# First value projection from un-normalized features, bias rows on GpSimd, first weight tile by ScalarE's queue

## The chip, the core and the metric

The kernel runs on one NeuronCore of a Trainium2 chip. TensorE (PE) multiplies matrices out of SBUF into PSUM, VectorE (DVE) and ScalarE (ACT) work element by element, GpSimd (POOL) does so too and issues DMAs, SyncE (SP) issues DMAs. Each engine runs its own instructions in program order and waits on semaphores for the others. The metric is the device time of one execution, in microseconds.

## What is computed

A trunk of two layers over x of 512 tokens and 1024 features, in float32. Cut to what matters here:

```python
def rmsnorm(x, g):
    y = x * lax.rsqrt(jnp.mean(x * x, axis=-1, keepdims=True) + EPS)
    return y * g

# layer 0, hgrn2_mixer; u = rmsnorm(x, ln_g[0]), W = 2048
q, f_pre, i_in, gate = u @ w_in[:, 0:W], u @ w_in[:, W:2*W], u @ w_in[:, 2*W:3*W], u @ w_in[:, 3*W:4*W]
f = lb + (1.0 - lb) * sigmoid(f_pre)        # lb from a softmax over hg_lb_logits
# chunkwise recurrence with q, k = 1 - f, log f and the values i_in; then
y = rmsnorm_per_head(o) * norm_g * silu(gate);  h = x + y @ w_out
# layer 1: dilated attention in three groups; its logits get a relative-position bias
bias = bias_table[bucket]                   # bucket: distance -> one of 32, masked outside the window
```

Two facts carry the change. The norm multiplies a token's row by one number, its reciprocal root mean square, so `(x * g) @ w`, scaled by that number per token afterwards, is `rmsnorm(x, g) @ w`. And each row of the bias table is a piecewise constant function of distance.

## The kernel before

Features lie on partitions: `hT` holds x transposed as 8 slices (k = 0..7) of 128 features by 512 tokens, and `u` the normalized features in two parts, `u["hi"]` (rounded by ACT) and `u["lo"]` (the rest, by DVE). Weights come the same way: SP loads a tile of 512 KB to one of four slots of `raw`, ACT writes `w["hi"]`, DVE `w["lo"]`. A product is three matmuls, hi·hi, hi·lo and lo·hi (`split_matmuls`, L440).

The program is written by hand as one sequence for each engine, so the order in the source is the order on the engine. Layer 0 goes over 4 quads of 4 heads. For a head three tiles F, Q and G are projected (`head_tile`, weights stationary, 24 matmuls each in two halves); the values of a whole quad are projected by four tiles of two k each, into four PSUM banks, one for each block of 128 tokens (`value_step` for the first quad, `values` for later ones; u stationary, 3 matmuls for a k and a token block s, 96 in all). The recurrence of a head runs between the tiles of the next one: its scores, updates, outputs and norm sum stand in `recurrence`.

The opening, which the change is about, is one chain:

- SP loads x in four tiles `nat` (512 KB each, with `ident` behind the first), then the parameters, then four weight tiles, then constants, one-hot table, mask and bias table.
- PE transposes x, 32 transposes of 128x128 (L572) in eight groups of four, and DVE copies each group to `hT` (L1140). ACT squares x (L814) and computes the reciprocal root per token (L817, L819). DVE spreads it over a diagonal `y_f` (L1135), and PE makes `rstd` of it by a product with ones (L579).
- `norm(0)` on DVE: for each k, `tmp = hT * gain * rstd` (L1101) and `u["lo"] = tmp - u["hi"]` (L1106), with ACT's `u_high` (L791) between; the first four weight splits (`first_hi` L807, `first_lo` L1091) are woven in.
- PE starts the first values when slice 0 is split (`u_ready`), and in their middle multiplies the bias table by the one-hot table (`bias_rows`, L516). DVE adds the mask (L1174), SP stores the result to DRAM (`ext_rows`), and GpSimd writes the tiles of bias from there (L418).
- DVE computes the lower bound `lb` and `oml` from the parameters (L1148 to L1169).

`tmp` has two buffers, so slice k of `tmp` waits for `u["lo"]` of slice k-2. `qx` is scratch for mask and bias rows first, and belongs to `decays` (the recurrence's operands) afterwards; `load_after` on SP reloads a slot as soon as its two parts are made, and the store of `ext_rows` stands in SP's sequence behind the reloads of the first four slots.

## Time and profile before

| what | us |
|---|---|
| median of three runs | 1649.3 |
| lowest and highest | 1648.06, 1650.33 |
| the profiled execution | 1648.23 |
| its span, first to last instruction | 1646.4 |
| PE busy in the span | 1625.8 |
| DVE busy | 812.3 |
| ACT busy | 645.4 |
| POOL busy | 20.8 |

Between the span and the profiled execution's own time lie 1.8 us before and behind the recorded instructions. In the timeline a row stands for one instruction or for several alike, with its start, the time until the last of them ends, its engine, line and tiles, and in brackets how long the engine had been idle and what ended that. Matmul rows overlap: one of 0.39 us is followed by the next after 0.23 us. In names of products the moving operand comes first: `proj<-w_hi,u_hi` is a product of the values (u stationary), `proj<-u_hi,w_hi` one of a head tile.

### The profile page before, as it was taken

How to read it: one execution, taken by the hardware profiler on the slowest of the kernel's cores; microseconds unless marked ns; L12 is line 12 of the kernel's file. 1: busy time of each engine (PE TensorE's matmuls, PEld its weight loads, DVE VectorE, ACT ScalarE, POOL GpSimd, SP SyncE). 2: the span in 40 equal slices, each digit the busy share in tenths (PEclk: the TensorE clock that was granted, in tenths of full speed). 3: DMA queues.
4: the chain of work that ended last, by engine and by line, in shares of the span. 5: the costliest groups of instructions: out<-in, count | busy, mean ns of one | idle time of the engine just before them, and what ended most of it. 6: DMA issues, size and time to landing. Idle time of an engine off the chain costs nothing.

```text
span 1646.4 us, 22077 instructions
## 1 busy us (share of the span) xinstructions
PE 1625.8 (99%) x8235; PEld 1387.1 (84%) x8235; DVE 812.3 (49%) x1414; ACT 645.4 (39%) x1096; POOL 20.8 (1%) x40
## 2 busy tenths in 40 slices
PE   7999999999999999999999999999999999999997
PEld 5888888888887998888998888898888889888886
DVE  6674675575677724444333444423344431444445
ACT  4553453453453534333232334332333332243333
POOL 0000000000000000000000000000000000000000
PEclk9999999999999999999999999999999999999999
DMA  6523223323221433333232343333323333433311
GB/s 216 166 78 102 77 76 89 89 77 87 79 77 52 128 90 96 84 84 84 65 115 80 95 97 84 71 102 91 97 66 84 95 71 90 125 94 85 77 51 65
DMA packets 247998, 149.47 MB, mean 91 GB/s; under 512 B 47040, under 2 KB 227648, under 8 KB 247920
## 3 DMA queue, kind: packets, MB, share of 16 engines
q1 hardware_dynamic: 203328, 139.69, 30.6%
q0 software_dynamic: 2608, 8.39, 1.5%
q10 hardware_dynamic: 41984, 0.27, 1.3%
q8 instruction: 59, 0.97, 0.2%
q14 instruction: 19, 0.16, 0.0%
HBM read 146.02 MB, written 6.50 MB: 93 GB/s over the span
## 4 chain that ended last, share of the span: by engine, by line
PE 97%; DVE 2%; ACT 1%; DMA 0%; issue 0%; DVEq 0%; SPq 0%
PE proj L440 81%; PE inner L726 3%; PE inner L440 3%; PE inner L694 2%; PE inner L714 2%; PE inner L682 1%; PE inner L598 1%; PE inner L621 1%; PE inner L624 1%; PE inner L610 1%; PE inner L603 0%; DVE v L1532 0%; PE inner L631 0%; DMA ident<-consts 0%; DVE hT L1140 0%; PE inner L632 0%
## 5 line engine op out<-in xcount | busy, mean ns | idle before, releaser
L1086 DVE TENSOR_TENSOR w_lo<-raw,w_hi 128x1024 fp32r<-128x1024 f32 x252 | 307.8, 1223 | 451.0 <-ACT w_hi L775 449.9
L440 PE MATMUL proj<-u_hi,w_hi 128*128 128x512 f32 x1280 | 509.3, 398 | 0.0
L440 PE MATMUL proj<-u_hi,w_lo 128*128 128x512 f32 x1280 | 499.8, 390 | 0.0
L440 PE MATMUL proj<-u_lo,w_hi 128*128 128x512 f32 x1280 | 498.4, 389 | 0.0
L775 ACT ACTIVATE w_hi<-raw 128x1024 fp32r<-128x1024 f32 x252 | 265.0, 1053 | 127.8 <-PE proj L440 117.0
L440 PEld LDWEIGHTS proj<-u_hi,w_lo 128*128 128x128 f32 x1280 | 240.2, 188 | 52.0
L440 PEld LDWEIGHTS proj<-u_lo,w_hi 128*128 128x128 f32 x1280 | 240.7, 188 | 48.1
L440 PEld LDWEIGHTS proj<-u_hi,w_hi 128*128 128x128 f32 x1280 | 240.5, 188 | 47.8 <-issue 0.4
L440 PE MATMUL proj<-w_hi,u_hi 128*128 128x512 f32 x440 | 177.3, 403 | 3.0 <-DVE u_lo L1106 3.0
L440 PE MATMUL proj<-w_lo,u_hi 128*128 128x512 f32 x440 | 174.6, 397 | 0.0
L440 PE MATMUL proj<-w_hi,u_lo 128*128 128x512 f32 x440 | 174.4, 396 | 0.0
L440 PEld LDWEIGHTS proj<-w_hi,u_hi 128*128 128x128 f32 x440 | 113.8, 259 | 14.4 <-issue 4.5
L440 PEld LDWEIGHTS proj<-w_hi,u_lo 128*128 128x128 f32 x440 | 113.9, 259 | 8.0
L1032 ACT ACTIVATE qk<-proj 128x512 f32<-128x512 f32 x96 | 57.1, 595 | 161.6 <-PE proj L440 161.5
L440 PEld LDWEIGHTS proj<-w_lo,u_hi 128*128 128x128 f32 x440 | 114.1, 259 | 7.1
L962 ACT ACTIVATE rows<-rows,negm 128x256 f32<-128x256 f32 (+1 forms) x128 | 61.8, 484 | 141.5 <-DVE negm L1430 131.2
L440 PE MATMUL proj<-y_hi,w_hi 128*128 128x512 f32 x256 | 101.0, 394 | 1.2 <-DVE sg L1190 0.7
L440 PE MATMUL proj<-y_hi,w_lo 128*128 128x512 f32 x256 | 99.7, 390 | 0.0
L440 PE MATMUL proj<-y_lo,w_hi 128*128 128x512 f32 x256 | 99.7, 389 | 0.0
L1286 DVE TENSOR_TENSOR hT<-hT,proj 128x512 f32<-128x512 f32 x80 | 54.4, 686 | 63.7 <-PE proj L440 63.5
L783 ACT ACTIVATE v<-proj 128x512 f32<-128x512 f32 x52 | 31.0, 596 | 121.2 <-PE proj L440 109.8
L440 PEld LDWEIGHTS proj<-y_hi,w_hi 128*128 128x128 f32 x256 | 48.1, 188 | 12.0 <-issue 2.5
(172 smaller groups left out, 1490.1 us busy)
## 6 DMA issues: line engine op xcount, KB each, us to landing
raw<-at_w_in SPq DMA_DIRECT2D x160, 512.0 KB, 4.1
raw<-hg_w_in SPq DMA_DIRECT2D x64, 512.0 KB, 4.2
raw<-hg_w_out SPq DMA_DIRECT2D x16, 512.0 KB, 3.6
raw<-at_w_out SPq DMA_DIRECT2D x16, 512.0 KB, 4.8
v<-x SPq DMA_DIRECT2D x4, 512.0 KB, 5.0
bias_tiles<-ext_rows POOLq DMA_DIRECT2D x1, 2048.0 KB, 11.9
bias_tiles<-ext_rows POOLq DMA_DIRECT2D x2, 1024.0 KB, 17.2
bias_n<-bias_tiles POOLq DMA_DIRECT2D x16, 128.0 KB, 4.4
```

Source lines behind the costliest of these rows:

```text
L440: ins = nc.tensor.matmul(bank[:, :], stationary(a), moving(b), start=(first and n == 0), stop=(last and n == 2))
L598: ins = nc.tensor.matmul(to, aft[:, b * P + c * CH:b * P + (c + 1) * CH], q_steps(b, 0, c, NC - c), start=True, stop=True)
L610: ins = nc.tensor.matmul(p_U[:, b * P:(b + 1) * P], kT[:, b, :], v_sb[0][:, b, h * P:(h + 1) * P], start=True, stop=True)
L694: ins = nc.tensor.matmul(p_S[r // 2][:, ((r % 2) * 2 + i) * P:((r % 2) * 2 + i + 1) * P], qk[:, 2 + 2 * i, s], qk[:, 3 + 2 * i, s], start= ...
L714: ins = nc.tensor.transpose(p_T[n % 2][:, (i % 4) * P:(i % 4 + 1) * P], src, ident[:, :])
L726: ins = nc.tensor.matmul(o, vals, pT[:, i, :], start=(i == 0), stop=(i == len(TILES) - 1), skip_group_check=True)
L775: nc.scalar.activation(w["hi"][:, slot, :], raw[:, slot, :], ACT.Copy).then_inc(hi_ready, 1)
L783: nc.scalar.activation(v_sb[group][:, s, :], value_bank(layer, q, e)[:, :], ACT.Copy, scale=cols[:, 8 + ST * group + s:9 + ST * group + s] ...
L962: nc.scalar.activation(probs[:, i, 0:n], probs[:, i, 0:n], ACT.Exp, bias=negm[:, i:i + 1], accum_out=stat[:, i // ST, 1, b:b + 1]).then_in ...
L1032: nc.scalar.activation(o, src, ACT.Copy, scale=QSCALE if i in (Q0, Q1, Q2) else 1.0)\
L1086: nc.vector.tensor_tensor(w["lo"][:, slot, :], raw[:, slot, :], w["hi"][:, slot, :].bitcast(F32), ALU.subtract).then_inc(w_ready, 1)
L1286: nc.vector.tensor_tensor(hT[:, k, :], hT[:, k, :], proj[bank][:, :], ALU.add)\
```

## The change

- **Loads.** ACT's queue loads the first weight tile at its very start; SP loads x, `ident`, the gains `ln_g` behind `ident`, then the other three weight tiles, and the other parameters after them. The one-hot table is gone, the mask goes straight to `ext_sb`, and the bias table comes with heads on partitions (4-byte elements).
- **Copies.** Transposes are ordered by halves of the features: four groups with k = 0..3, then four with k = 4..7, and ACT, not DVE, copies them to `hT` (`x_copy`).
- **First values.** DVE makes `tmp = hT * gain` by blocks of 4 slices by 128 tokens (`x_gain`), ACT and DVE split them (`x_high`, `x_low`), and the first values are multiplied from these; `copy_values` scales them per token. PE runs 7 + 8 + 2 products of ones into a bank that nobody reads, before and between the first transposes.
- **Norm behind it.** `norm(0)` runs as before, but each pair of slices of `u` is written only when the values' tile that reads it is done. Splits of the next weight tiles, `lb` and `oml` stand in or behind it. The first head tile waits for each slice (`u_ready`).
- **Bias rows.** GpSimd adds the bias, one instruction for each run of equal bucket (53 runs on 16 partitions by 1 to 30 elements), to the mask in place; `bias_rows` and DVE's three additions are gone. `decays` waits for the store of these rows.

```diff
@@ sync
             load_x(0)
             sp.dma_start(ident[:, :], consts[:, 0:P]).then_inc(const_loaded[0], 16)
+            sp.dma_start(prow[0:16, P:2 * P], ln_g.rearrange("r (h p) -> (r h) p", p=P)).then_inc(const_loaded[3], 16)
             for t in range(1, ST):
                 load_x(t)
+            for n in range(1, SLOTS):
+                load(n, *tile_source(HG, 0, "value", 0, n))
...
-                    sp.wait_ge(ext_ready, GROUPS)
+                    sp.wait_ge(ext_ready, 1)
@@ gpsimd
+            pool.wait_ge(const_loaded[5], 16)
+            pool.wait_ge(const_loaded[6], 16)
+            for g, bucket, first, count, step in bias_runs():
+                run = slice(g * EXT + first, g * EXT + first + (count - 1) * step + 1, step)
+                ins = nc.gpsimd.tensor_scalar(ext_sb[:, run], ext_sb[:, run],
+                                              relb_sb[:, bucket * GROUPS + g:bucket * GROUPS + g + 1], None, ALU.add)
+            ins.then_inc(ext_ready, 1)
@@ tensor, value_step
-                if s == 0 and layer is HG:
-                    pe.wait_ge(u_ready, k + 1)
+                if layer is HG and k % 4 == 0:
+                    pe.wait_ge(raw_ready, k + s + 1)
@@ scalar
             def u_high(which, k):
-                if which:
-                    wait_tile_done(act, AT, None, 4 + k // 2, False)
+                wait_tile_done(act, AT if which else HG, None, 4 * which + k // 2, False)
...
+            act.dma_start(raw[:, 0, :].rearrange("p (k n) -> p k n", k=2),
+                          w_in[HG][:, 0:2, HG_VALUE[0]:HG_VALUE[0] + HQ * P]).then_inc(loaded[0], 16)
...
+            x_square(0)
+            x_copy(0)
+            first_hi(0)
+            x_high(0)
+            x_copy(1)
+            x_copy(2)
+            x_high(1)
+            first_hi(1)
+            x_copy(3)
+            x_high(2)
+            x_high(3)
+            x_square(1)
+            x_copy(4)
+            x_square(2)
+            x_square(3)
...
+            x_copy(5)
+            x_high(4)
@@ vector, norm
+                    if not which and k == 2:
+                        split_lo(HG, None, 0, False)
+                    if not which and k == KT - 2:
+                        split_lo(HG, None, 1, False)
+                        split_lo(HG, None, 2, False)
+                        dve.wait_ge(param_T, 1)
+                        nc.vector.tensor_copy(param[:, 0:64], inner[1][:, 0:64]).then_inc(param_ready, 1)
...
+            def x_gain(n):
+                half = n // ST
+                dve.wait_ge(x_copied, n + 1)
+                if n >= 2:
+                    dve.wait_ge(raw_ready, n - 1)
+                nc.vector.tensor_tensor(tmp[:, n % 2, :].rearrange("p (a b) -> p a b", b=P), block(hT, n),
+                                        param[:, 64 + 4 * half:68 + 4 * half].unsqueeze(2).broadcast_to([P, 4, P]),
+                                        ALU.mult).then_inc(xg_made, 1)
...
@@ vector, decays
                 dve.wait_ge(eb_ready, 2 * g + 2)
+                dve.wait_ge(ext_stored, 16)
```

PE's sequence at its start, before. `v` is x as loaded, `inner` and `proj` are PSUM banks:

```order
L572 MATMUL inner<-ident,v 128x128 x32
L576 MATMUL proj<-ident,rows 128x80
L579 MATMUL inner<-y_f,ones 128x512
L440 MATMUL proj<-w_hi,u_hi 128x512
L440 MATMUL proj<-w_lo,u_hi 128x512
L440 MATMUL proj<-w_hi,u_lo 128x512
```

And PE's sequence at the same place in the changed kernel (L448 is `split_matmuls`, L582 the transposes, L567 and L572 the products of ones):

```order
L567 MATMUL proj<-ones 128x128 x7
L582 MATMUL inner<-ident,v 128x128 x4
L588 MATMUL inner<-ident,rows 128x16
L572 MATMUL proj<-ones 128x128 x8
L582 MATMUL inner<-ident,v 128x128 x4
L572 MATMUL proj<-ones 128x128 x2
L582 MATMUL inner<-ident,v 128x128 x4
L448 MATMUL proj<-w_hi,u_hi 128x512
L448 MATMUL proj<-w_lo,u_hi 128x512
L448 MATMUL proj<-w_hi,u_lo 128x512
```

The products of the values now stand behind twelve transposes where thirty-two stood before, and the other twenty, with the product that makes `rstd`, stand between them.

DVE's sequence behind its first copies, before, up to the second split of a weight tile:

```order
L1143 COPY param<-proj 128x80
L1091 TENSOR_TENSOR w_lo<-raw,w_hi 128x1024
L1101 SCALAR_TENSOR_TENSOR tmp<-hT,param,rstd 128x512 x2
L1106 TENSOR_TENSOR u_lo<-tmp,u_hi 128x512
L1101 SCALAR_TENSOR_TENSOR tmp<-hT,param,rstd 128x512
L1106 TENSOR_TENSOR u_lo<-tmp,u_hi 128x512
L1091 TENSOR_TENSOR w_lo<-raw,w_hi 128x1024
```

DVE's sequence in the changed kernel from block 5 of `x_gain` to the start of `norm(0)` (L1217 `x_gain`, L1224 `x_low`, L1163 `first_lo`, L1173 the first step of the norm):

```order
L1217 TENSOR_TENSOR tmp<-hT,param 128x512 x2
L1224 TENSOR_TENSOR u_lo<-tmp,u_hi 128x4x128
L1244 TENSOR_TENSOR y_f<-ident,cols 128x512
L1217 TENSOR_TENSOR tmp<-hT,param 128x512
L1224 TENSOR_TENSOR u_lo<-tmp,u_hi 128x4x128
L1217 TENSOR_TENSOR tmp<-hT,param 128x512
L1224 TENSOR_TENSOR u_lo<-tmp,u_hi 128x4x128
L1163 TENSOR_TENSOR w_lo<-raw,w_hi 128x1024
L1224 TENSOR_TENSOR u_lo<-tmp,u_hi 128x4x128
L1163 TENSOR_TENSOR w_lo<-raw,w_hi 128x1024
L1173 SCALAR_TENSOR_TENSOR tmp<-hT,param,rstd 128x512 x2
```

The norm, which stood almost first on DVE, now stands behind sixteen block operations, four splits and the diagonal.

## Rows read from the trace of the kernel before

**Rows 1.** The page, part 1 (PE, DVE, POOL) and part 4 (the chain that ended last).

```profile
PE 1625.8 (99%) x8235; PEld 1387.1 (84%) x8235; DVE 812.3 (49%) x1414; ACT 645.4 (39%) x1096; POOL 20.8 (1%) x40
...
PE 97%; DVE 2%; ACT 1%; DMA 0%; issue 0%; DVEq 0%; SPq 0%
```

**Rows 2.** Windows: stretch, length, busy of each engine, granted clock, DMA share, GB/s.

```profile
8.00:15.50 7.50, 3.56 (x23) 2.53 (x22) 7.40 (x12) 5.03 (x10) 0.00 (x0) 0.97 1.06 368
15.50:21.80 6.30, 5.85 (x14) 4.62 (x15) 6.23 (x9) 3.85 (x6) 0.00 (x0) 0.50 0.70 163
21.80:43.00 21.20, 21.20 (x91) 16.04 (x90) 13.28 (x27) 7.93 (x12) 3.23 (x3) 1.00 0.57 176
```

**Rows 3.** Timeline: loads of x, squares on ACT, transposes, and the product for `rstd`.

```profile
0.88 0.39 SPq L364 DMA_DIRECT2D v<-x  x1
...
4.94 1.06 ACT L814 ACTIVATE qk<-v 128x1024 f32<-128x1024 f32 x1 [2.77 <-DMA v<-x]
...
5.19 5.17 PE L572 MATMUL inner<-ident,v 128*128 128x128 f32 x32 [5.19 <-DMA ident<-consts]
...
5.90 0.19 ACT L814 ACTIVATION_READ_ACCUMULATOR qk<-v 128x1 f32 x1
...
9.03 1.06 ACT L814 ACTIVATE rows<-v 128x1024 f32<-128x1024 f32 x1 [0.22 <-DMA v<-x]
...
11.79 1.13 PE L579 MATMUL inner<-y_f,ones 128*128 128x512 f32 x2 [1.36 <-DVE y_f L1135]
```

**Rows 4.** Timeline: the first slice's split, the first product of the values, and its successor.

```profile
15.11 0.69 DVE L1106 TENSOR_TENSOR u_lo<-tmp,u_hi 128x512 fp32r<-128x512 f32 x1
15.65 1.05 ACT L807 ACTIVATE w_hi<-raw 128x1024 fp32r<-128x1024 f32 x1
15.84 0.75 DVE L1101 SCALAR_TENSOR_TENSOR tmp<-hT,param,rstd 128x512 f32<-128x512 f32 x1
...
15.95 0.76 PE L440 MATMUL proj<-w_hi,u_hi 128*128 128x512 f32 x1 [3.04 <-DVE u_lo L1106]
...
16.51 0.68 DVE L1106 TENSOR_TENSOR u_lo<-tmp,u_hi 128x512 fp32r<-128x512 f32 x1
...
16.63 0.63 ACT L791 ACTIVATE u_hi<-tmp 128x512 fp32r<-128x512 f32 x1
...
17.12 1.22 DVE L1091 TENSOR_TENSOR w_lo<-raw,w_hi 128x1024 fp32r<-128x1024 f32 x1
```

**Rows 5.** Timeline: first and last DVE steps of the norm.

```profile
13.67 1.41 DVE L1101 SCALAR_TENSOR_TENSOR tmp<-hT,param,rstd 128x512 f32<-128x512 f32 x2
...
26.49 1.48 DVE L1106 TENSOR_TENSOR u_lo<-tmp,u_hi 128x512 fp32r<-128x512 f32 x2
```

**Rows 6.** Timeline: the values' product ahead of the bias rows and the one behind them.

```profile
29.50 0.39 PE L440 MATMUL inner<-w_hi,u_lo 128*128 128x512 f32 x1
...
31.85 0.50 PE L440 MATMUL proj<-w_hi,u_hi 128*128 128x512 f32 x1
```

**Rows 7.** Timeline: PE begins the first and the second head tile.

```profile
42.91 0.39 PE L440 MATMUL proj<-u_hi,w_hi 128*128 128x512 f32 x1
...
48.35 0.39 PE L440 MATMUL proj<-u_hi,w_hi 128*128 128x512 f32 x1
```

**Rows 8.** Timeline: GpSimd's only instructions that write SBUF.

```profile
0.48 0.10 POOL L1569 MEMSET const-uint8-127<- 128x1 uint8 x1
0.87 0.20 POOL L406 MEMSET ones<- 128x128 f32 x1 [0.29 <-POOLq L1569]
```

**Rows 9.** Timeline: first recurrence, on DVE its operands, on PE its scores.

```profile
54.98 0.69 DVE L1242 TENSOR_TENSOR qx<-proj,rows 128x512 f32<-128x512 f32 x1
...
58.43 0.42 DVE L1255 TENSOR_TENSOR qx<-qx,rows 128x256 f32<-128x256 f32 x1
...
62.04 1.06 PE L598 MATMUL inner<-qx,aft 128*32 128x128 f32 x32
```

**Rows 10.** DMA issues: the last constants and the store of bias rows, us to landing.

```profile
bias_n<-rel_bias SPq DMA_DIRECT2D x1, 6.0 KB, 9.0
...
ext_rows<-qx SPq DMA_DIRECT2D x1, 72.0 KB, 2.0
```

More of the change, by code:

```diff
@@ L23 @@
+import itertools
 from contextlib import ExitStack
@@ L563, in _ @@
             pe.wait_ge(ones_ready, 1)
+            for _ in range(7):
+                nc.tensor.matmul(proj[2][:, 0:P], ones[:, :], ones[:, :], start=True, stop=True)
             pe.wait_ge(const_loaded[0], 16)
[L565 to L573 removed]
@@ L574, in _, with idle_products, x_transposes @@
-            for i in (1, 2, 3):
-                pe.wait_ge(const_loaded[i], 16)
-            nc.tensor.transpose(proj[0][:, 0:80], prow[0:80, 0:P], ident[0:80, 0:80]).then_inc(param_T, 1)
+            def idle_products(n):
+                for _ in range(n):
+                    nc.tensor.matmul(proj[2][:, 0:P], ones[:, :], ones[:, :], start=True, stop=True)
+            def x_transposes(half, t):
+                n = ST * half + t
+                if half == 0:
+                    pe.wait_ge(x_loaded[t], 16)
+                if n >= 3:
+                    pe.wait_ge(x_copied, n - 2)
+                for i in range(4):
+                    ins = nc.tensor.transpose(inner[1 + n % 3][:, i * P:(i + 1) * P],
+                                              nat[t][:, half, i * P:(i + 1) * P], ident[:, :])
+                ins.then_inc(x_T, 1)
@@ L647, in hg_body @@
                     for half in range(2 * HG.per_head):
-                        head_tile(HG, q, HG.per_head * h + half // 2, half % 2)
+                        head_tile(HG, q, HG.per_head * h + half // 2, half % 2, first=(h == 0 and half < 2))
                         if h:
@@ new lines, in x_low @@
+            def x_low(n):
+                dve.wait_ge(raw_hi_ready, n + 1)
+                nc.vector.tensor_tensor(block(u["lo"], n), tmp[:, n % 2, :].rearrange("p (a b) -> p a b", b=P),
+                                        block(u["hi"], n).bitcast(F32), ALU.subtract).then_inc(raw_ready, 1)
+            dve.wait_ge(gain_T, 1)
+            nc.vector.tensor_copy(param[:, 64:80], p_ss[:, 64:80]).then_inc(gain_ready, 1)
+            dve.wait_ge(gain_ready, 1)
+            x_gain(0)
+            first_lo(0)
@@ L1145, in _ @@
+            x_gain(6)
+            x_low(5)
+            x_gain(7)
+            x_low(6)
+            first_lo(2)
+            x_low(7)
+            first_lo(3)
+            dve.wait_ge(raw_ready, KT)
+            norm(0)
             dve.wait_ge(param_ready, 1)
-            norm(0)
             nc.vector.tensor_tensor(lb[:, :], param[:, 0:H], param[:, H:2 * H], ALU.max).then_inc(lb_step, 1)
@@ L1543, in bucket_of, with distance, bias_runs @@
     return np.where(dist < exact, dist, np.minimum(large, BUCKETS - 1))
+def distance(g, e):
+    window, dilation = ((128, 1), (512, 4), (2048, 16))[g]
+    apart = 2 * P - 1 - e
+    dist = apart * (1 if g == 0 else RES)
+    return dist if apart >= 0 and dist % dilation == 0 and dist <= window else None
+def bias_runs():
+    for g in range(GROUPS):
+        step = RES if g == 2 else 1
+        seen = [e for e in range(EXT) if distance(g, e) is not None]
+        for bucket, run in itertools.groupby(seen, lambda e: int(bucket_of(np.array(distance(g, e))))):
+            run = list(run)
+            assert run == list(range(run[0], run[-1] + 1, step))
+            yield g, bucket, run[0], len(run), step
 def shape_constants():
@@ L1551, in shape_constants @@
     consts[:, 2 * P:] = (np.arange(S) % CH != 0)
-    onehot = np.zeros((BUCKETS, GROUPS, EXT), np.float32)
     relmask = np.full((H, GROUPS, EXT), MASKED, np.float32)
-    for g, (window, dilation) in enumerate(((128, 1), (512, 4), (2048, 16))):
-        order = 1 if g == 0 else RES
+    for g in range(GROUPS):
         for e in range(EXT):
-            apart = 2 * P - 1 - e
-            dist = apart * order
-            if apart >= 0 and dist % dilation == 0 and dist <= window:
-                onehot[bucket_of(np.array(dist)), g, e] = 1.0
+            if distance(g, e) is not None:
                 relmask[:, g, e] = 0.0
-    return consts, onehot.reshape(BUCKETS, -1), relmask.reshape(H, -1)
+    return consts, relmask.reshape(H, -1)
 def kernel(**inputs):
```

181 lines of the change are left out of this document (103 added, 78 removed).

## The prediction, made before the changed kernel ran

> **What bounds the kernel now.** The page first: PE is busy for 99% of the span and is 97% of the chain that ended last [rows 1]. A microsecond that PE gains at the start is one for the kernel, as long as what follows doesn't wait for something else; DVE and ACT, each under half busy over the whole, can bound it only locally. So I read the opening in the timeline. PE transposes from 5.19 as x lands [rows 3], and begins the values only at 15.95, 0.15 after DVE has split the first slice (15.11 + 0.69) [rows 4]. From there it has no gap but one of bias rows until the head tiles, which begin at 42.91 and 48.35 [rows 7]. Those two starts are my markers: all that the change touches lies before 48.35, and behind it both kernels do the same matmuls. The windows show the clock [rows 2]: granted 0.97 up to 15.5, when PE had been idle for most of 5 us, then 0.50 (the lower level, 1.2 GHz) for 6.3 us with 14 products, then 1.00 (2.4 GHz). At full clock a product of 512 columns follows another after 0.227 us ((48.35 - 42.91) / 24) [rows 7]; in the slow stretch it took 5.85 / 14 = 0.42 [rows 2].
>
> **Steps on each engine.** Rows of one instruction overlap the next by a tenth, so I price by starts. DVE by 512 elements: 0.61 to 0.67, I take 0.65 (15.84 to 16.51 to 17.12); DVE by 1024: 1.22, 1.17 as a step; ACT by 512: 0.63, a step of 0.57; ACT by 1024: 0.98 (15.65 to 16.63) [rows 4]. A square with its sum: 5.90 + 0.19 - 4.94 = 1.15, I take 1.2 [rows 3]. Four transposes: 5.17 / 8 = 0.65 while PE also waited for copies; I take 0.5 [rows 3].
>
> **Loads.** x(0) was issued at 0.88 and ACT had it at 4.94; x(3) came at 9.03, so 512 KB take (9.03 - 4.94) / 3 = 1.36 us with the DMA engines full [rows 3]. The changed kernel issues the first weight tile at the same moment from another queue. The DMA share was 1.06 of the engines in the stretch around the loads [rows 2], so nothing is left to share out: the two together take 2.7 us where one took 1.3, and x(0) lands between 4.94 (it goes ahead) and 6.3. I take 6.2, because both queues start at once, and the weights land with it. The Trainium skill, "DMA: Bandwidth & Descriptors", section "Issuing engines are not separate DMA queues", says that DMAs of all issuing engines run on the same 16 and interleave; by that rule too x(0) is late, and if it did not hold, x(0) would stay at 4.94 and the total below 1.3 us lower.
>
> **ACT up to the second half of x.** In its order: square, copy (7.4 to 8.0), first weight split (to 9.0), `x_high(0)` (to 9.5), and on the other side DVE's `x_gain(0)` at 8.05, the weight's low part (to 10.2), `x_low(0)` (to 10.85). So PE's first product of the values is at 10.98: 4.97 earlier than 15.95. But ACT has more ahead of the second half: up to the end of `x_copy(5)` 4 squares (4.8), 6 copies and 4 `x_high` (5.7), 2 weight splits (2.0), one small one (0.3) and some 1.05 of waits for DVE and PE: 6.2 + 13.9 = 20.1.
>
> **DVE from there.** `x_gain(5)` must wait for that copy. Then DVE has 8 steps of 0.65 and 2 of 1.17 to the start of the norm: 20.1 + 7.6 = 27.7. The norm is the same chain as before, 8 steps of `tmp`, 8 of `u["lo"]`, 3 weight splits: it took from 13.67 to 26.49 + 1.48 = 27.97, that is 14.3 [rows 5], with a copy of parameters (0.2) now 14.5. It ends at 42.3, and slice 6, one step ahead of the last, is split at 41.7.
>
> **PE.** From 10.98: eight value steps of 3 products (5.5), transposes between them (4 groups, 2.0), waits for `x_low` of 0.45, then k = 2 with the last group (3.2), the product for `rstd` (1.0; it took 1.13 [rows 3]) and a wait of 0.1, twenty value steps (13.6), one small transpose (0.15): 37.05, where the first head tile can begin. Before it was 42.91. As a sum of differences: the start -4.97; the slow clock, if it doesn't return, 14 x (0.42 - 0.227) = -2.7 [rows 2]; bias rows gone from PE, -(31.85 - 29.50 - 0.23) = -2.1 [rows 6]; five groups of transposes +2.5, the product and small transpose +1.2, waits +0.55. That is -5.5 by rounded terms, -5.86 laid out step by step; the difference is in PE's first products at the change of clock. Now the norm comes too: the head tile wants slice 6 at 37.05 + 18 x 0.227 = 41.15 and gets it at 41.83 (41.7 and a hop), a stall of 0.7. The second head tile begins at 37.05 + 5.45 + 0.7 = 43.2 instead of 48.35: **-5.15 us without any interference**. DVE is from here the bound: each microsecond that it loses in the norm is lost one for one.
>
> **GpSimd beside DVE.** 53 instructions start when mask and bias table have landed. The bias table came 9.0 after its issue at 8.72 [rows 10], so about 17.5. No row shows such an instruction, nor DVE beside it. The nearest are memsets: 0.10 for one column, 0.20 for 128 [rows 8]. If they share nothing with DVE the cost is 0. If each takes something from DVE, 53 x 0.10 = 5.3 us is the row's upper figure if all of it fell on DVE, and twice that by the other memset. I expect a part only: DVE idles from about 17.5 to 20.1, where a good number go free, and of the rest each DVE step meets at most one. I take 0.05 on each of the 28 large steps from 20.1 to 42: +1.4. It can't be below nothing, since nothing leaves DVE's norm for it (the three additions came behind the norm).
> The Trainium skill speaks against this part: "SBUF — State Buffer", section "Who interferes with whom", has VectorE instructions with two SBUF inputs and GpSimd instructions that read SBUF exclude each other for a whole instruction, whichever began first. All of DVE's block and norm steps have two such inputs. No row here shows it; by the rule the term is above zero, without it the sum would be -5.15.
>
> **What costs nothing.** The products of ones run while PE would wait for x and for `x_low(0)`: 17 small ones, 3.6 us at full clock, in a stretch that begins at 1.1 and has PE idle for 4; if that cover is gone (x lands at 4.94) the eight of them delay the second transposes by under 1 us, with ACT not yet there. The eight waits on `u_ready` at each quad's first tile ride on matmuls and are long fulfilled. The store wait in `decays` stands ahead of all of DVE's recurrence: it needs GpSimd done and 2.0 us for the store [rows 10]. `decays` began at 54.98 [rows 9]; everything being earlier, it comes now at about 52.4 by DVE's own order (the lower bound, one split and a memset moved behind the norm delay it by some 2.5 us against the head tile). Scores were wanted at 62.04 and their operands were ready at 58.43 + 0.42 = 58.85 [rows 9], a reserve of 3.2. Of it 2.5 are used up; 0.7 stay.
>
> **The time.** -5.15 + 1.4 = -3.75. The profiled execution took 1648.23, 1.1 under the median of 1649.3; the difference goes against either alike: 1648.23 - 3.75 = 1644.5, and 1649.3 - 3.75 = 1645.55. I state the latter.
>
> **Rivals.**
> 1. *The full gain.* GpSimd takes nothing from DVE: -5.15, 1644.15; with x(0) at 4.94 it is -6.4, 1642.9. For it: sixteen partitions and few elements. Against: nothing measured either way. Chance 0.22.
> 2. *The forecast*, -2.9 to -4.6: 1644.7 to 1646.4. Chance 0.38.
> 3. *DVE loses 0.1 or more per step, or the clock falls again.* At 0.1 on 28 steps it is +2.8, -2.35, 1646.95; at 0.2, +5.6, +0.45, 1649.75. If PE is granted 0.5 for a stretch like the one before while it works on the values, it loses up to 2.7 us, 0.7 of which the stall of the first head tile absorbs: -3.1 alone, -1.9 with a little of the other. For it: between 5.19 and 15.5 PE's work was nearly all transposes and the clock fell behind it [rows 2, 3]; the same kind of work with pauses precedes the values now. Against: 17 real products were added among them, and the idle stretch is shorter. 1646.4 to 1650. Chance 0.30.
> 4. *Slower: GpSimd holds SP and DVE.* The store of bias rows waits for all 53; SP's next weight load stands behind it, and `decays` in DVE. It decides where `ext_ready` comes later than about 50: (50 - 17.5) / 53 = 0.6 us for each instruction. If each has to wait behind a DVE step of 0.65 to 1.17 and DVE leaves no pause, that is the rate; at 1.0 they end at 70.5, the store at 72.5, and the recurrence is 20 us late, of which the reserve covers 0.7: +19 - 5, 1663. The same rival in a milder form is a DVE loss of 0.3 per step: +8.4 - 5.15 = +3.3, 1652.6. Against: DVE is nearly idle after 45 and GpSimd catches up. Chance 0.07.
> 5. *It isn't kept.* The recurrence of the first head, started 2.5 us later against its tiles, makes PE wait and gives back 1 to 3: -1 to -3, 1646.3 to 1648.3. Chance 0.03.
>
> **Range and chances.** 0.2% of 1649.3, 3.3 us, is about what a measurement can tell from no change. Rival 1 and the better 0.30 or so of the forecast are beyond it: faster 0.52. The rest of the forecast, most of rival 3 and rival 5: same 0.40. Slower 0.08. The range leaves out rival 4, half of the ends of 1 and 3: 1642.9 to 1649.3.
>
> **What would show it.** PE's first values product near 11.0 and x(0) seen by ACT near 6.2; no stretch at 0.5 after 11; DVE's norm from 27.7 to 42 or a little more, steps of 0.70 instead of 0.65 while GpSimd works; head tiles at 37 and 44.6 on PE, the stall in the first before its slices 6 and 7; `ext_rows` stored before 50; scores of the first head without a wait. The prediction is wrong if DVE's steps beside GpSimd take 0.8 and more, if the granted clock is 0.5 while the values run, or if the second head tile is early and the span isn't.

## The result

The changed kernel takes 1657.6 us (median of five runs, 1656.1 to 1658.1) against 1649.3: 1.0050 of the kernel before, 95% interval 1.0036 to 1.0064. It is slower by 8.3 us. The profiled execution has a span of 1656.2 where the kernel before had 1646.4, 9.8 more. Parts 1 and 4 of its page, to be read beside [rows 1]:

```profile
PE 1629.7 (98%) x8264; PEld 1391.0 (84%) x8264; DVE 816.2 (49%) x1420; ACT 653.6 (39%) x1112; POOL 54.1 (3%) x93
...
PE 93%; POOL 2%; DMA 2%; DVE 2%; ACT 1%; SPq 1%; issue 0%; DVEq 0%
```

GpSimd is busy 33 us longer, and 2% of the chain that ended last, some 33 us, lie on it. Nothing of it stood on that chain before. Yet the opening came out near the forecast, in part by errors that cancel (see below). The timeline of the changed kernel, the rows that answer to [rows 3, 4, 7]:

```profile
4.88 1.06 ACT L862 ACTIVATE qk<-v 128x1024 f32<-128x1024 f32 x1 [2.21 <-DMA v<-x]
...
10.27 0.47 PE L448 MATMUL proj<-w_hi,u_hi 128*128 128x512 f32 x1
...
38.03 0.50 PE L448 MATMUL proj<-u_hi,w_hi 128*128 128x512 f32 x1 [0.81 <-ACT v L816]
...
43.60 0.39 PE L448 MATMUL proj<-u_hi,w_hi 128*128 128x512 f32 x1
```

The values begin at 10.27 instead of 15.95, the second head tile at 43.60 instead of 48.35: 4.75 us won. What came then is in the windows (stretch, length, busy of PE, PEld, DVE, ACT, POOL, granted clock, DMA share, GB/s):

```profile
46.00:52.00 6.00, 6.00 (x29) 4.95 (x28) 1.15 (x3) 1.36 (x2) 6.00 (x20) 1.00 0.01 3
52.00:58.00 6.00, 5.37 (x24) 4.12 (x22) 0.00 (x0) 0.09 (x1) 3.60 (x6) 1.00 0.59 157
58.00:64.00 6.00, 0.00 (x0) 0.00 (x0) 4.35 (x7) 4.06 (x6) 0.35 (x1) 0.61 1.08 360
64.00:70.00 6.00, 4.12 (x40) 3.40 (x41) 4.96 (x12) 1.79 (x3) 0.00 (x0) 0.54 0.97 315
```

From 52 to 58 DVE and ACT do nothing, from 58 to 64 PE does nothing, and behind it the granted clock is at its lower level. DMA moves 3 GB/s from 46 to 52: no weight tile is on its way. The timeline tells why (GpSimd's additions and SP's store, the loads behind it, ACT and DVE waiting, and PE's scores):

```profile
19.53 4.76 POOL L420 TENSOR_SCALAR qx<-qx,bias_n 16x30 f32<-16x30 f32 x5 [18.44 <-DMA bias_n<-rel_bias]
...
52.67 0.34 SPq L385 DMA_DIRECT2D ext_rows<-qx  x1
53.45 28.61 SPq L342 DMA_DIRECT2D raw<-hg_w_in  x8
...
57.91 1.06 ACT L808 ACTIVATE w_hi<-raw 128x1024 fp32r<-128x1024 f32 x1 [10.30 <-DMA raw<-hg_w_in]
...
59.51 1.23 DVE L1332 TENSOR_TENSOR_SCAN rows<-restart,rows 128x512 f32<-128x512 f32 x1 [10.73 <-ACT rows L980]
...
65.88 1.92 PE L631 MATMUL inner<-qx,aft 128*32 128x128 f32 x32 [8.51 <-DVE qx L1357]
```

The 53 additions last from 19.53 to the store at 52.67, 0.62 us each. SP waits for them, and its next weight load, behind that wait, goes out at 53.45. ACT's split of that tile stands ahead of its logarithm of the forget gate, which DVE's scan needs, which the scores need. In the kernel before, the scores stood at 62.04 without a wait [rows 9]. Here 4.75 us of lead turned into 3.84 of lag. The second head's scores come at 92.54 against 82.70 (PE, the kernel before and then the changed one):

```profile
82.70 1.06 PE L598 MATMUL inner<-qx,aft 128*32 128x128 f32 x32
```

```profile
82.09 0.50 PE L664 MATMUL inner<-osq_hi,ones_r 128*128 128x512 f32 x1 [2.47 <-DVE osq_lo L1371]
...
92.54 1.06 PE L631 MATMUL inner<-qx,aft 128*32 128x128 f32 x32
```

So 6.0 us more were lost between the two, 2.5 of them as a wait of the first norm sum, and the rest behind the two waits, where the granted clock is low (0.54 from 64 to 70 above, 0.72 from 82 to 88). From there the two kernels run alike: 9.84 at these scores, 9.8 at the end.

This gives a reading that serves for every run below: the start of the second head tile says what the opening is worth, and the span less that start what was lost behind it. Both come from one profiled execution, the median from all. It is 1598.05 for the kernel before and 1612.6 for the changed one.

### The profile page after: what moved, and what is told of

Its sections match the earlier page's. It is cut to its first block, busy times and chain, and to the rows that moved or that the text cites. A ratio compares the mean times of both kernels' runs of the same rounds, so it can differ in the third digit from the quotient of the medians.

```text
span 1656.2 us, 22236 instructions
## 1 busy us (share of the span) xinstructions
PE 1629.7 (98%) x8264; PEld 1391.0 (84%) x8264; DVE 816.2 (49%) x1420; ACT 653.6 (39%) x1112; POOL 54.1 (3%) x93
## 4 chain that ended last, share of the span: by engine, by line
PE 93%; POOL 2%; DMA 2%; DVE 2%; ACT 1%; SPq 1%; issue 0%; DVEq 0%
PE proj L448 78%; PE inner L759 3%; PE inner L448 3%; POOL qx L420 2%; PE inner L727 2%; PE inner L747 2%; PE inner L715 1%; DMA raw<-hg_w_in 1%; PE inner L631 1%; PE inner L654 1%; DMA bias_n<-rel_bias 1%; PE inner L657 1%; PE inner L643 1%; PE inner L636 0%; DVE v L1634 0%
## 5 line engine op out<-in xcount | busy, mean ns | idle before, releaser
L448 PE MATMUL proj<-u_hi,w_hi 128*128 128x512 f32 x1280 | 510.4, 399 | 0.8 <-ACT v L816 0.8
L448 PE MATMUL proj<-u_hi,w_lo 128*128 128x512 f32 x1280 | 500.5, 391 | 0.0
L448 PE MATMUL proj<-u_lo,w_hi 128*128 128x512 f32 x1280 | 499.2, 390 | 0.0
L448 PEld LDWEIGHTS proj<-u_hi,w_lo 128*128 128x128 f32 x1280 | 240.8, 188 | 52.3
L448 PEld LDWEIGHTS proj<-u_hi,w_hi 128*128 128x128 f32 x1280 | 241.1, 188 | 48.9 <-ACT v L816 1.2
L448 PEld LDWEIGHTS proj<-u_lo,w_hi 128*128 128x128 f32 x1280 | 241.3, 188 | 48.3
L448 PE MATMUL proj<-w_hi,u_hi 128*128 128x512 f32 x440 | 177.2, 403 | 1.0 <-DVE u_lo L1224 0.9
L448 PE MATMUL proj<-w_lo,u_hi 128*128 128x512 f32 x440 | 173.7, 395 | 0.0
L448 PE MATMUL proj<-w_hi,u_lo 128*128 128x512 f32 x440 | 173.7, 395 | 0.0
L448 PEld LDWEIGHTS proj<-w_hi,u_hi 128*128 128x128 f32 x440 | 113.3, 258 | 11.4 <-DVE w_lo L1158 2.1
L448 PEld LDWEIGHTS proj<-w_hi,u_lo 128*128 128x128 f32 x440 | 113.4, 258 | 7.8
L448 PEld LDWEIGHTS proj<-w_lo,u_hi 128*128 128x128 f32 x440 | 113.6, 258 | 7.0 <-issue 0.2
L448 PE MATMUL proj<-y_hi,w_hi 128*128 128x512 f32 x256 | 100.9, 394 | 1.2 <-DVE sg L1291 0.7
L448 PE MATMUL proj<-y_hi,w_lo 128*128 128x512 f32 x256 | 99.8, 390 | 0.0
L448 PE MATMUL proj<-y_lo,w_hi 128*128 128x512 f32 x256 | 99.7, 389 | 0.0
L448 PEld LDWEIGHTS proj<-y_hi,w_hi 128*128 128x128 f32 x256 | 48.1, 188 | 12.0 <-issue 2.5
```

The source lines that it names most:

```text
L448: ins = nc.tensor.matmul(bank[:, :], stationary(a), moving(b), start=(first and n == 0), stop=(last and n == 2))
```

## The experiments

Twelve kernels ran, all in five rounds, in three groups of four; the kernels of a group and the kernel before ran on the same chip. The ratio is against the kernel before on that chip (1648.7, 1648.3 and 1648.9 in the three groups), with its 95% interval.

| kernel | median | ratio (interval) | second head tile | span less that |
|---|---|---|---|---|
| before | 1649.3 | 1 | 48.35 | 1598.05 |
| changed | 1657.6 | 1.0050 (1.0036 to 1.0064) | 43.60 | 1612.6 |
| `half_runs` | 1650.1 | 1.0006 (0.9996 to 1.0015) | 45.49 | 1602.5 |
| `pool_store` | 1649.0 | 0.9998 (0.9988 to 1.0007) | 45.43 | 1602.6 |
| `old_bias` | 1651.9 | 1.0022 (1.0013 to 1.0031) | 45.29 | 1603.8 |
| `before_plus53` | 1649.0 | 1.0000 (0.9991 to 1.0009) | 49.86 | 1597.5 |
| `late_write` | 1653.2 | 1.0031 (1.0020 to 1.0042) | 44.17 | 1606.3 |
| `half_late` | 1644.5 | 0.9975 (0.9965 to 0.9985) | 44.69 | 1598.1 |
| `own_scratch` | 1644.2 | 0.9974 (0.9965 to 0.9984) | 45.58 | 1598.5 |
| `best53` | 1643.5 | 0.9971 (0.9960 to 0.9981) | 43.53 | 1597.6 |
| `best38` | 1644.0 | 0.9969 (0.9957 to 0.9980) | 44.27 | 1598.2 |
| `best_sp_load` | 1647.6 | 0.9993 (0.9984 to 1.0002) | 47.73 | 1598.2 |
| `best_no_ones` | 1644.2 | 0.9972 (0.9961 to 0.9983) | 44.27 | 1597.9 |
| `best53_again` | 1643.6 | 0.9968 (0.9956 to 0.9980) | 44.23 | 1597.7 |

The second head tile moves by up to 2 us between profiles of kernels with the same opening (43.53 and 44.23 for the same kernel). The last section says what goes with it. The last column of that kernel hardly moves (1597.6 and 1597.7).

### Fewer additions: `half_runs`

```diff
-            for g, bucket, first, count, step in bias_runs():
+            for g, bucket, first, count, step in list(bias_runs())[:27]:
```

> The changed kernel with only the first 27 of GpSimd's 53 bias instructions (the bias is left out of the other runs, so it computes something else there). Theory A, the store of the bias rows comes too late and SP's next weight load stands behind it: in the changed kernel 53 instructions ran from 19.53 to 52.64; 27 end near 38.5, before ACT wants the next weight tile at 47.6, so the 8.5 us wait of the first scores is gone, with the slow clock behind it, and the 4.75 us won up to the second head tile stay: about 1644.6. Theory B, what is late is the lower bound and the recurrence's start on DVE, moved behind the norm: GpSimd's count changes nothing, the scores still wait 5 us or more and the time stays above 1653.

The 8.5 us wait is gone, as theory A has it, and so theory B in its strong form is out: what was late at the scores was the store. But A's number was missed by 5.5 us. The 27 additions end at 44.05 and not near 38.5: they took 0.93 us each, since nearly all of them lie beside DVE's blocks and norm. The second head tile is 1.9 us later than in the changed kernel's profile. And PE waits at another place (the waits of PE in `half_runs`: line, who ended the wait, us, times, longest; then GpSimd and ACT in its timeline):

```profile
PE inner L664 <- DVE osq_lo L1371: 2.7, 1, 2.7
```

```profile
46.44 3.31 POOL L426 DMA_DIRECT2D bias_tiles<-ext_rows  x3 [2.40 <-DMA ext_rows<-qx]
...
69.34 1.06 ACT L808 ACTIVATE w_hi<-raw 128x1024 fp32r<-128x1024 f32 x1 [3.32 <-DMA raw<-hg_w_in]
```

ACT waits 3.3 us for a weight tile, and in its shadow the norm sum is late. From 46.44 GpSimd writes the bias tiles, 4 MB from DRAM to DRAM. In the kernel before it did so at 34.85, with SP's loads four slots ahead. Here those loads had been held until 44.85. A second theory had to be added to A: the writes meet loads that are already late. `late_write` and `half_late` test it.

### SP's queue freed: `pool_store`

```diff
@@ sync
-                if layer is HG:
-                    sp.wait_ge(ext_ready, 1)
-                    sp.dma_start(ext_dram.rearrange("g h e -> h g e"),
-                                 ext_sb.rearrange("h (g e) -> h g e", g=GROUPS)).then_inc(ext_stored, 16)
@@ gpsimd
+            pool.wait_ge(ext_ready, 1)
+            pool.dma_start(ext_dram.rearrange("g h e -> h g e"),
+                           ext_sb.rearrange("h (g e) -> h g e", g=GROUPS)).then_inc(ext_stored, 16)
```

> The changed kernel with all 53 instructions, but GpSimd itself issues the store of the bias rows, so that SP's weight loads don't stand behind it; DVE's wait for the store stays. Theory A1 (SP's queue is what costs): the weight tile is there in time, the decays start when the store has landed, near 55.7, their operands are ready at 59.6, the scores are wanted at 57.3: a wait of 2.3 instead of 8.5, and about 1646.8. Theory A2 (DVE's own wait for the store costs as much as SP's queue): the scores wait 8 us as before and it is about 1657.

The scores wait 2.9 us instead of 8.5, near A1's 2.3, and ACT doesn't wait for a weight tile:

```profile
62.06 1.06 PE L630 MATMUL inner<-qx,aft 128*32 128x128 f32 x32 [2.86 <-DVE qx L1356]
```

So DVE's own wait for the store is good for 2.9 us, and SP's queue, which lasts longer, for the rest of the 8.5. The median is 2.2 above A1's number. In spans, where both ends are profiled executions, it is 4.05 (1648.0 against 1646.4 - 4.75 + 2.3): 0.6 us of longer wait, 1.6 lost between the two heads' scores (84.30 - 62.06 = 22.24 against 20.66), with a granted clock of 0.78 from 60 to 66, which A1 hadn't counted, and 1.8 of a later opening.

### Bias rows back on PE and DVE: `old_bias`

```diff
+            bias_rows()
             for k in (5, 6, 7):
...
@@ vector, behind the lower bound
+            dve.wait_ge(const_loaded[6], 16)
+            for g in range(GROUPS):
+                dve.wait_ge(ext_done, g + 1)
+                nc.vector.tensor_tensor(ext_sb[:, g * EXT:(g + 1) * EXT], inner[1 + g][0:H, 0:EXT],
+                                        relmask_sb[:, g * EXT:(g + 1) * EXT], ALU.add).then_inc(ext_ready, 1)
```

> The changed kernel with the bias rows made as before, by three products on PE behind the fifth k of the values and three additions on DVE behind the lower bound; everything else as changed. Theory A: nothing is late, PE pays the 2.1 us of its three products against the 4.75 won: -2.6, about 1646.7; the scores don't wait. Theory B (start of the recurrence moved too late on DVE, here with 1.7 us more of additions in front): the scores wait 2 us or more and the time is 1649 or above.

Both theories missed something. The time is on theory B's side of the line, but the scores wait only 1.1 us; another product waits 1.0 for ACT, and the norm sum 3.0. With no addition on GpSimd the bias rows are still late, because DVE's additions stand behind the norm, which now stands behind the values' splits. SP's loads wait for them just so; ACT waits for weight tiles three times, 11.0 us in all. The granted clock stays at 1.00 behind these waits. Putting the rows back on PE doesn't bring the kernel below the one before. The rows are ready late here as in the changed kernel, and the same loads queue behind them: moving the additions off GpSimd alone doesn't mend that.

### GpSimd beside DVE: `before_plus53`

```diff
+            pool.wait_ge(ones_ready, 1)
+            pool.wait_ge(const_loaded[7], 16)
+            at = 0
+            for g, bucket, first, count, step in bias_runs():
+                nc.gpsimd.tensor_scalar(scratch[:, at:at + count], ones[0:H, 0:count],
+                                        ones[0:H, bucket:bucket + 1], None, ALU.add)
+                at += count
```

> The kernel before, with 53 GpSimd instructions of the same shapes added (ones plus ones into a scratch tile that nobody reads), started when the bias table has landed, ahead of GpSimd's writes of the bias tiles, which come some 15 us later for it; output unchanged. Theory C, GpSimd and DVE hold each other up, and DVE loses: DVE's steps of the norm take 0.70 and more a start instead of 0.65, its norm ends 1 to 3 us later than at 27.97, and with a late norm PE starts no later but its values stall. Theory D, only GpSimd waits: DVE's steps and end as before, GpSimd's instructions 0.7 us each beside a busy DVE and 0.3 beside an idle one, time 1649.3 within 1.

Theory D: no difference, 1649.0 against 1648.7 on the same chip. DVE's norm takes 14.3 us, from 15.40 to 28.27 + 1.47, as it did alone [rows 5], with GpSimd at work beside it from 18.93 on:

```profile
15.40 1.41 DVE L1110 SCALAR_TENSOR_TENSOR tmp<-hT,param,rstd 128x512 f32<-128x512 f32 x2
...
28.27 1.47 DVE L1115 TENSOR_TENSOR u_lo<-tmp,u_hi 128x512 fp32r<-128x512 f32 x2
```

It also shows that writing the bias tiles some 11 us later isn't dear by itself: SP's loads weren't held there. In the changed kernel the same holds for DVE; its groups in 20 to 42, with GpSimd at work all the time, have the mean times of the kernel before (687 and 685 ns a step):

```profile
L1178 DVE TENSOR_TENSOR u_lo<-tmp,u_hi 128x512 fp32r<-128x512 f32 x8 | 5.5, 687 | 0.3 <-ACT u_hi L823 0.2
```

```profile
L1106 DVE TENSOR_TENSOR u_lo<-tmp,u_hi 128x512 fp32r<-128x512 f32 x5 | 3.4, 685 | 0.1
```

GpSimd pays instead. The changed kernel's GpSimd, beside a busy DVE and then beside an idle one:

```profile
22.96 25.50 POOL L420 TENSOR_SCALAR qx<-qx,bias_n 16x10 f32<-16x10 f32 x35
47.94 4.70 POOL L420 TENSOR_SCALAR qx<-qx,bias_n 16x1 f32<-16x1 f32 x15
```

That is 25.5 / 35 = 0.73 and 4.7 / 15 = 0.31 us each. But the first stretch mixes two prices. Cut at DVE's norm, which ends at 41.66, it is 1.1 us each beside the norm (the row of 7) and 0.45 beside the short steps that follow (the row of 12):

```profile
29.31 7.89 POOL L420 TENSOR_SCALAR qx<-qx,bias_n 16x1 f32<-16x1 f32 x7
```

```profile
40.93 5.41 POOL L420 TENSOR_SCALAR qx<-qx,bias_n 16x1 f32<-16x1 f32 x12
```

`before_plus53` says the same: 1.2 us each beside DVE's norm, 0.47 behind it:

```profile
18.93 10.89 POOL L421 TENSOR_SCALAR scratch<-ones 16x30 f32<-16x30 f32 x9 [17.84 <-DMA bias_n<-rel_bias]
```

```profile
29.01 7.44 POOL L421 TENSOR_SCALAR scratch<-ones 16x1 f32<-16x1 f32 x16
```

So theory D's 0.7 beside a busy DVE was too low for the norm. Width explains little of it: in the changed kernel additions of one column take 1.10 us each from 29.3 to 37 (8 of them) and 0.32 from 48 to 53 (6 of them), where one of 13 columns takes 0.36. Nor does ACT: from 42 to 46 of `before_plus53` ACT is busy for 3.17 us and DVE for 0.18, and 15 instructions run in those 4 us. The Trainium skill, "SBUF — State Buffer", section "Who interferes with whom", says that the two exclude each other for an instruction where VectorE has two SBUF inputs and GpSimd reads SBUF, the later one waiting. The GpSimd side of the trace agrees (1.1 to 1.2 us against 0.3); on DVE's side nothing of it can be seen.

### Bias tiles written late: `late_write` and `half_late`

```diff
             pool.wait_ge(ext_stored, 16)
+            pool.wait_ge(O_done, HQ)
```

> The changed kernel, with GpSimd's three writes of the bias tiles (4 MB from DRAM to DRAM, not read before the attention) held back until the first quad's four outputs are done. Theory A says that two things were lost behind the second head tile: the wait of the first scores (8.5 us) on the store and on the weight load queued behind it, and then, at the first norm sum, 2.5 us with a slow clock behind it, because those 4 MB run against the weight loads that are late already. Here the first stays and the second goes: scores wait 8.5, norm sum none: 1657.6 less 2.5 to 4, about 1654. Theory E (the norm sum is late only because the loads were issued late, whatever else moves): it still waits 2 us or more, and the time stays at 1657.

> 27 of GpSimd's 53 bias instructions (the others' bias is left out) and the bias tiles written late. With 27 instructions alone the scores didn't wait but the norm sum waited 2.7 us and the clock fell behind it; nothing was left of the 4.75 us. Theory A: with the 4 MB out of the way the norm sum doesn't wait either, and the gain of the opening stays: 4 us or more below the kernel before, 1644.5. Theory E: the norm sum waits as it did, and the time is about that of the kernel before.

Theory A with its second part, in both. In `late_write` the scores wait 6.9 us, the norm sum doesn't wait, and the time is 1653.2 where 1654 was expected. Of the loss behind the second head tile, 14.6 - 8.3 = 6.3 us are gone (1612.6 against 1606.3 in the last column), 1.6 of them in the shorter wait at the scores: SP's load went out at 52.45 instead of 53.45, and the second head tile came 0.6 later. That is from one profile each; the medians differ by 4.4. `half_late` keeps the whole gain: 1644.5, the number expected, and a last column of 1598.1, that of the kernel before. Against `half_runs` one line differs, and it is worth 4.4 us in the last column (1602.5 to 1598.1). The held loads didn't go out earlier for it: at 44.48, 0.2 us ahead of the second head tile, against 44.85, 0.6 ahead. Theory E is out.

### Nobody waits: `own_scratch` and `best53`

`own_scratch` has `pool_store` and this:

```diff
-        ext_sb = qx_flat[0:H, 0:GROUPS * EXT]
+        ext_sb = qk[:, 3:6, :].rearrange("p a b -> p (a b)")[0:H, 0:GROUPS * EXT]
...
-                dve.wait_ge(ext_stored, 16)
...
             quads(act, hg_body)
+            act.wait_ge(ext_stored, 16)
```

(`qk` is not used before the attention; the squares' output, which nobody reads, went there and moved.) `best53` adds the late writes.

> The changed kernel with all 53 instructions, the mask and the bias rows in a tile that the recurrence doesn't use (so the decays don't wait for the store), and GpSimd issuing the store (so SP's loads don't either); the bias tiles are written as soon as the rows are stored, near 56. Theory A: the scores don't wait; the 4 MB come when four weight tiles are already ahead, so they may cost 0 to 3 us: between 1644.5 and 1647.5. Theory B (the recurrence's start on DVE is late by itself): the scores wait 1 us or more with neither wait left.

> The same with the bias tiles written late as well: all 53 instructions, nobody waiting for them in the first quad. Theory A: PE has no wait between the second head tile and the first quad's end, and the whole gain of the opening stays: 4.4 to 4.75 us below the kernel before, 1644.5, ratio 0.9972. Theory B: 1647 or above, with a wait at the scores.

Both as theory A expects. GpSimd needs even longer, nearly 40 us in `best53`, and nobody minds:

```profile
19.30 39.72 POOL L416 TENSOR_SCALAR qk<-qk,bias_n 16x30 f32<-16x30 f32 x53 [18.22 <-DMA bias_n<-rel_bias]
```

```profile
43.53 0.39 PE L448 MATMUL proj<-u_hi,w_hi 128*128 128x512 f32 x1
...
57.23 1.06 PE L631 MATMUL inner<-qx,aft 128*32 128x128 f32 x32
```

The scores come 13.7 us behind the second head tile, as in the kernel before (62.04 - 48.35), without a wait. Theory B is out altogether: the recurrence's start on DVE isn't late by itself. In `own_scratch`, where the 4 MB are still written at 59.98, the scores don't wait either (59.27 - 45.58 = 13.69). With four slots loaded ahead the 4 MB cost some 0.8 us, if anything (the medians 1644.2 and 1643.5, whose intervals overlap). `best53` is 4.9 us faster than the kernel before.

### What the other parts are worth: `best38`, `best_sp_load`, `best_no_ones`

Three changes of `best53`: sixteen additions of one column each replaced by one that reads the table backwards; the first weight tile loaded by SP; no products of ones.

```diff
@@ best38
+            nc.gpsimd.tensor_tensor(cells, cells, table, ALU.add)
@@ best_sp_load
-            act.dma_start(raw[:, 0, :].rearrange("p (k n) -> p k n", k=2),
-                          w_in[HG][:, 0:2, HG_VALUE[0]:HG_VALUE[0] + HQ * P]).then_inc(loaded[0], 16)
...
-            for n in range(1, SLOTS):
+            for n in range(SLOTS):
@@ best_no_ones
-            for _ in range(7):
-                nc.tensor.matmul(proj[2][:, 0:P], ones[:, :], ones[:, :], start=True, stop=True)
...
-            idle_products(8)
-            idle_products(2)
```

> The kernel with a scratch tile of its own, GpSimd's store and the late writes (1643.5, 4.9 below the kernel before), with sixteen of the 53 GpSimd instructions, one column each, replaced by one addition that reads the table backwards: 38 in all. Nobody waits for them any more, so no difference: within 1 us of 1643.5. GpSimd's span shrinks from 39.7 us to about 28. If GpSimd did cost DVE anything, a third fewer instructions would show as 0.5 us or more below it, and DVE's norm would end earlier.

> The same kernel with all 53, but the first weight tile loaded by SP's queue behind x and the gains, ahead of the other weight tiles, instead of by ACT's queue at the start. The tile then lands some 5 us later (behind three loads of x at 1.36 us, near 10.4 instead of 5.8), x(0) somewhat earlier if the two loads had shared the DMA engines. PE's first product of the values, which waits for the tile's two parts, comes some 3 us later; ACT and DVE, which wait for it in order, shift by about as much. Expected 1 to 3 us above 1643.5. If the load cost x(0) as much as it gave, no difference.

> The same kernel with all 53 and ACT's load, without the 17 products of ones that PE runs before and between the first transposes. If they keep the clock up, the granted clock is 0.5 for a stretch while the values run, as in the kernel before (14 products at 0.42), and the second head tile comes up to 2.7 us later: 1644.5 to 1646. If the values' own products are enough, no difference.

> The same kernel with all 53 once more, as the reference of this chip for the three others: 4 to 5 us below the kernel before, ratio 0.997.

`best38`: no difference, and GpSimd is done 28.7 us after it began. `best_sp_load` is 4.0 us above `best53_again`, more than expected, and that is three quarters of the gain of 5.3 on that chip. PE waits 4.1 us for its first product:

```profile
13.68 0.77 PE L448 MATMUL proj<-w_hi,u_hi 128*128 128x512 f32 x1 [4.10 <-DVE u_lo L1223]
```

And behind that wait the clock is low, which the expectation hadn't counted: granted 0.50 from 14 to 16 and 0.51 to 17, while the first six products of the values run 0.43 us apart instead of 0.23, some 1.2 us in all. This is the prediction's rival 3, in another kernel.

The load costs x(0) little (ACT's first square in `best_sp_load`, and in `best53_again`):

```profile
4.27 1.06 ACT L860 ACTIVATE qk<-v 128x1024 f32<-128x1024 f32 x1 [2.11 <-DMA v<-x]
```

```profile
4.88 1.06 ACT L862 ACTIVATE qk<-v 128x1024 f32<-128x1024 f32 x1 [2.22 <-DMA v<-x]
```

That is 0.6 us; the kernel before, with no such load beside it, saw x(0) at 4.94 [rows 3]. But what stands behind x(0) in SP's queue pays the whole share. `ident` lands 4.7 us after its issue instead of 3.1, and PE's first transpose, which waits for it, comes at 6.09 instead of 4.47; the four tiles of x land after 6.2 instead of 4.8 us (medians).

`best_no_ones` is 0.6 above `best53_again`, with intervals that overlap, and its second head tile comes at 44.27 against 44.23: whether the products of ones bring anything isn't settled. They do change the start of the values. Without them the first product comes at 10.85 instead of 11.57, but from 11.41 to 12.69 they follow one another after 0.43 us instead of 0.23. The granted clock reads 1.00 there all the same, while in the kernel before the same pace, 0.42, stood at 0.50 [rows 2]. So that column can't be relied on for the first microseconds of a trace.

## Why the prediction was wrong, point by point

**Loads.** x(0) was seen at 4.88, not 6.2: it didn't share with ACT's load as forecast. What follows x(0) did: `ident` let PE's first transpose go at 6.03 where the kernel before had 5.19. So ACT's copy began at 6.72, 0.7 earlier than the 7.4 of the working, and not 1.3, and the values began at 10.27 instead of 10.98.

**ACT, DVE and PE up to the second head tile.** Right in kind, and the number, 43.60, lies between the 43.2 without interference and the 44.6 with it. That is partly luck. The start was 0.7 early, DVE's norm too (26.98, forecast 27.7), and the norm took 14.7 (14.5). As PE came 1.0 us later than the working's 37.05, it no longer met the norm's end, and the stall of 0.7 in the first head tile wasn't there. PE was later because it needed 27.8 us from its first product of the values to the first head tile at 38.03, where the working had 26.1: 0.8 of it as a wait for a bank that ACT still copied, which the working didn't have, as `x_copy` and the values' copies had been laid out by duration, without the bank they free; 0.4 in longer waits for `x_low` (0.9 against 0.45). The rest wasn't followed up.

**The products of ones** weren't free. Eight of them stand ahead of the second transposes and take 2.05 us here, and up to 3.78 in other runs with this opening; the last section has them.

**GpSimd beside DVE.** The term was laid on the wrong engine. +1.4 us was put on DVE, and DVE lost nothing; GpSimd lost 0.8 to 0.9 us an instruction beside the norm. The price of an instruction was taken from memsets of 0.10 and 0.20 us, which read nothing. An addition took 0.31 beside an idle DVE and 1.1 beside its norm, 0.62 over all: three to eleven times the row used.

**The store wait in `decays`, and the load behind the store.** This is the step that failed. "What costs nothing" has the store wait "needs GpSimd done and 2.0 us for the store", and rests on GpSimd being done early, with no time worked out for it, and it gives SP's next weight load behind the store no term at all. The runs showed this in its place: by the measured price GpSimd ends at 19.5 + 53 x 0.625 = 52.6, the load goes out at 53.45, ACT waits 10.3 us for it and PE 8.5 at the scores. With the store off SP's queue (`pool_store`) 2.9 of these 8.5 are left, and with scratch of its own (`own_scratch`) none.

**Rival 4** named the mechanism, its places (SP's load behind the store, DVE's wait) and its point of decision, 0.6 us for each instruction. It was 0.62. It got 0.07 because its price was compared with the memsets, and because DVE was expected to be idle after 45. That part came true, 0.3 us each there, and it is why the mean was 0.62 and not the 1.1 beside the norm. At that mean its own arithmetic gave little: ready at 52.6 instead of 50, some 2.6 us less the reserve. The wait was 8.5. It was too coarse in two ways. The deadline is that of the load behind the store (ready 4.5 us before ACT wants the tile at 47.6, so 43, or 0.44 us for each instruction), not that of the store. And ACT's queue turns a late weight tile into a late logarithm.

**Not there at all**: the 4 MB of bias tiles as a thing that moves. The prediction counted the store of 72 KB, and not what GpSimd issues behind it. It cost 4.4 to 4.7 us with the clock behind it (last column, `late_write` and `half_late` against their partners, less the shorter wait). A moved step moves every DMA behind it on its queue.

**Slow clock.** Rival 3 placed it in the values, where it didn't come in the changed kernel. It came behind the two waits of PE in the recurrence, granted 0.54 from 64 to 70 and 0.72 from 82 to 88. `late_write`, which has the first wait alone, lost 1.9 us between the two heads' scores (87.38 - 64.84 = 22.54 against 20.66); by that the second cost 1.6 (6.0 - 2.5 - 1.9). It doesn't follow every wait: `old_bias` waits 3.0 us and is granted 1.00 behind it.

**The reserve** of the first recurrence was there, and larger than the 0.7 us counted: ACT's tile was 10.3 us late and the scores 8.5, so 1.8. With nobody holding it up PE doesn't wait (`best53`).

## What to carry to other kernels

When work moves to an engine whose instructions the trace doesn't show, multiply the count by a price that is several times too high, and look where its end stands against the first waits behind it. Here there was room for 0.44 us each, and it was 0.62. A wait put into an in-order load queue has the deadline of the next load behind it, not of what it waits for, and a long transfer that is issued behind the wait comes late as well and runs into the loads that now have no lead. Both are mended without touching the slow part: let the engine that makes the data issue its store, and give it scratch that nobody else wants (`own_scratch`, 1644.2). Where loads have no lead, hold back transfers that aren't needed for a while (`half_late`); where they have it, that brought little (`best53`, 1643.5).

## What was not expected of the hardware

GpSimd's small additions hardly depend on their width and strongly on VectorE. Beside an idle one they take 0.32 us for one column and 0.36 for 13; beside its norm 1.1 to 1.2 for one column. VectorE's steps stay at 0.685 to 0.687 with and without them.

The bias table with 4-byte elements, 6 KB in 1536 pieces, seems to be a heavy transfer for its size. The windows of the changed kernel around it:

```profile
14.00:15.00 1.00, 0.27 (x3) 0.03 (x1) 1.00 (x2) 0.76 (x2) 0.00 (x0) 1.00 1.13 345
15.00:16.00 1.00, 0.84 (x4) 0.71 (x5) 0.90 (x3) 1.00 (x2) 0.00 (x0) 1.00 1.37 96
16.00:17.00 1.00, 1.00 (x8) 0.82 (x7) 1.00 (x2) 1.00 (x4) 0.00 (x0) 1.00 1.25 58
```

The DMA engines are full and move 58 to 96 GB/s where they moved 345, for some 3 us. That it is this table is inferred from its place behind the last large loads; no run took it away alone. `old_bias` loads it in whole rows, with the one-hot table beside it, and moves 210 and 149 GB/s from 15 to 17, at shares of 1.18 and 1.11. So a part of the slump belongs to the small constants in any form.

PE's first products are slow though the granted clock reads 1.00. Seven products of ones, 14 records, take 3.35 us at 1.14, 0.24 each, and the next eight at 6.78, 16 records, 2.05, 0.13 each:

```profile
1.14 3.35 PE L567 MATMUL proj<-ones 128*128 128x128 f32 x14 [1.14 <-POOL ones L406]
...
6.03 0.66 PE L582 MATMUL inner<-ident,v 128*128 128x128 f32 x4 [1.54 <-DMA ident<-consts]
...
6.78 2.05 PE L572 MATMUL proj<-ones 128*128 128x128 f32 x16
```

How long the eight take differs from run to run, and the second transposes stand behind them. In `half_runs`, whose second head tile comes at 45.49, it was:

```profile
7.26 3.78 PE L572 MATMUL proj<-ones 128*128 128x128 f32 x16
```

Among the kernels with this opening and GpSimd's additions the two go together: 2.05 us and a second head tile at 43.5 to 43.6 (changed, `best53`); 2.87 to 3.17 and 44.2 to 44.3 (`late_write`, `best38`, `best53_again`); 3.58 and 44.7 (`half_late`); 3.78 and 45.4 to 45.6 (`half_runs`, `pool_store`, `own_scratch`). Without any of them it was 44.27 (`best_no_ones`). So by these profiles they cost more than they bring when they are slow; why they are slow in one run and not in another isn't shown. An opening is worth comparing over many runs only.
